# The delta rule of a two-block layer stack over chunks of 128 tokens in place of 64

## The reference

```
lower = strict_lower((beta k) k^T * decay)          # C x C
u, w  = solve(I + lower, [beta v, beta k exp(gc)])   # unit lower triangular
intra = lower_incl(q k^T * decay)
per chunk, in order:
    v_new = u - w S
    o     = (q exp(gc)) S + intra v_new
    S     = S exp(g_last) + (k exp(g_last - gc))^T v_new
```

## Time and profile before

| | |
|---|---|
| median of 3 runs | 2641.05 us |
| the profiled execution | 2638.55 us |
| its span in the profile | 2636.4 us |
| mean granted TensorE clock | 0.977 |
| TensorE matmul busy | 2543.8 us (96%) |
| VectorE busy | 1718.5 us (65%) |
| ScalarE busy | 1226.5 us (47%) |
| DMA | 428.50 MB, mean 163 GB/s |

### The profile page before, as it was taken

The page is one execution under the profiler, slowest core; times in us unless marked ns, Lnnn a source line. Parts: engine busy times, 40 slices in busy tenths (PEclk is TensorE's granted clock), DMA queues, the critical chain, the costliest instruction groups (busy, mean ns, idle before and its releaser), DMA issues.

```text
span 2636.4 us, 39407 instructions
## 1 busy us (share of the span) xinstructions
PE 2543.8 (96%) x17188; PEld 2337.9 (89%) x17188; DVE 1718.5 (65%) x1888; ACT 1226.5 (47%) x1275; POOL 0.2 (0%) x4
## 2 busy tenths in 40 slices
PE   7999999899998998999999999999899999999997
PEld 7998888789998978799999989987799999898876
DVE  5699855755888737565655657556656756577664
ACT  5544224554452225554334333337456556455573
POOL 0000000000000000000000000000000000000000
PEclk8999989999999979999999999999999999999999
DMA  5453222355442213455555555555445555545553
GB/s 209 166 178 129 96 79 89 136 192 180 175 175 95 86 61 112 165 204 179 186 183 191 178 190 188 183 201 199 159 176 176 179 189 176 185 180 179 183 193 119
DMA packets 63212, 428.50 MB, mean 163 GB/s; under 512 B 6976, under 2 KB 7104, under 8 KB 13504
## 3 DMA queue, kind: packets, MB, share of 16 engines
q1 hardware_dynamic: 60496, 414.97, 44.3%
q10 hardware_dynamic: 2544, 11.01, 1.1%
HBM read 421.76 MB, written 4.19 MB: 162 GB/s over the span
## 4 chain that ended last, share of the span: by engine, by line
PE 84%; DVE 6%; ACT 6%; issue 3%; DMA 0%; ACTq 0%; DVEq 0%; SPq 0%
PE PS L406 83%; ACT Q L878 2%; DVE Q L1456 2%; ACT WH L892 1%; DVE WL L1491 1%; PE PS L496 1%; DVE QA L1460 1%; ACT L878 1%; DVE Y L1456 1%; ACT QA L878 1%; DVE X L1460 1%; DVE Q L1460 0%; ACT HH L878 0%; PE PS L692 0%; DVE QA L1456 0%
## 5 line engine op out<-in xcount | busy, mean ns | idle before, releaser
L1491 DVE TENSOR_TENSOR WL<-W,WH 128x2048 fp32r<-128x2048 f32 (+2 forms) x388 | 861.2, 2224 | 544.1 <-ACT WH L892 544.0
L892 ACT ACTIVATE WH<-W 128x2048 fp32r<-128x2048 f32 (+2 forms) x388 | 717.5, 1858 | 779.8 <-PE PS L406 666.6
L406 PE MATMUL PS<-HH,WL 128*128 128x256 f32 x3392 | 564.2, 286 | 17.2 <-DVE WL L1491 12.1
L406 PE MATMUL PS<-HL,WH 128*128 128x256 f32 x3392 | 557.6, 284 | 0.0
L406 PE MATMUL PS<-HH,WH 128*128 128x256 f32 x3392 | 557.1, 284 | 0.0
L406 PEld LDWEIGHTS PS<-HH,WL 128*128 128x128 f32 x3392 | 474.0, 193 | 24.8 <-DVE WL L1491 12.7
L406 PEld LDWEIGHTS PS<-HL,WH 128*128 128x128 f32 x3392 | 473.3, 193 | 0.0
L406 PEld LDWEIGHTS PS<-HH,WH 128*128 128x128 f32 x3392 | 472.9, 193 | 0.0
L406 PE MATMUL PS<-WL,HH 128*128 128x512 f32 (+2 forms) x768 | 231.0, 382 | 10.0 <-DVE HL L1456 10.0
L406 PE MATMUL PS<-WH,HL 128*128 128x512 f32 (+2 forms) x768 | 223.7, 372 | 0.0
L406 PE MATMUL PS<-WH,HH 128*128 128x512 f32 (+2 forms) x768 | 222.7, 371 | 0.0
(11 more groups left out here) (135 smaller groups left out, 1990.1 us busy)
## 6 DMA issues: line engine op xcount, KB each, us to landing
W<-in_wall SPq DMA_DIRECT2D x378, 1024.0 KB, 4.8
W<-in_wall SPq DMA_DIRECT2D x16, 512.0 KB, 3.5
W<-in_wall SPq DMA_DIRECT2D x8, 536.0 KB, 3.4
X<-in_x SPq DMA_DIRECT2D x4, 512.0 KB, 7.4
X<-in_x ACTq DMA_DIRECT2D x1, 2048.0 KB, 10.2
xsave<-X ACTq DMA_DIRECT2D x1, 2048.0 KB, 10.7
X<-xsave ACTq DMA_DIRECT2D x1, 2048.0 KB, 11.0
Q<-in_g_post ACTq DMA_DIRECT2D x8, 256.0 KB, 3.3
```

The costliest lines, as they stand in the source:

```text
L406: return e.matmul(o, l, r, start=start, stop=stop, skip_group_check=True)
L892: e.activation(WH[:, s % NSPL, 0:m], W[:, c % NRAW, 0:m], ACT.Copy).then_inc(*up("hi", c))
L1491: e.tensor_tensor(WL[:, c % NRAW, 0:m], W[:, c % NRAW, 0:m], WH[:, s % NSPL, 0:m].bitcast(F32), ALU.subtract).then_inc(*up("lo", c))
```

## The change

The constants' masks lose the blocks of 64 (`cum`, `incl`, `strict`; `last` becomes `ones`), and there is a sixth level, 128. The scan has two steps: in the first S is zero, so its `v_new` is `U2` itself, its state is the product `kv` alone, copied by ScalarE, and its output is one product; the second makes `ws`, `vn` and an output of two products, and no further state. `wk`, `EG`, `CQ`, `RW` and `KD` are made only for the half that is read. TensorE's wait for `kb` ahead of `kk` stands four pumps later, the `tu` transposes two later in all, and attention's `kr` wait three pumps later on TensorE and ScalarE. VectorE's counts stay but for the sixth level and the scan.

```diff
-    same = (i[:, None] // 64) == (i[None, :] // 64)
-    c["cum"] = same & (i[:, None] <= i[None, :])
+    c["cum"] = i[:, None] <= i[None, :]
...
+        def three(ap):
+            return ap[:, 0:384].rearrange("p (h c) -> p h c", h=3)
...
-        LEVELS = (4, 8, 16, 32, 64)
+        LEVELS = (4, 8, 16, 32, 64, 128)
...
# TensorE
-                yield from rest(4)
+                yield from rest(8)
                 for k in range(3):
                     for which, rhs_ in (("kk", KB), ("kq", CQ)):
...
                     yield
-                yield from rest(4)
+                yield from rest(2)
                 for k in range(3):
                     b = side(("dn", l, "tu", k), ("dn_a", l, "tu", k))
...
-                        for which in ("u", "t") if m < 64 else ("u",):
+                        for which in ("u", "t") if m < 128 else ("u",):
...
+                for k in range(2):
+                    b = side(("dn", l, "wk", k), ("dn_a", l, "wk", k))
+                    for h in range(3 * k, 3 * k + 3):
+                        us = slice(256 * h + 128, 256 * h + 256)
+                        i = mm(b[:, 128 * (h % 3):128 * (h % 3) + 128], RW[:, us], UU[:, us], start=(h % 3 == 0))
...
                 yield from rest(2)
-                for c in range(4):
...
+                w.wait_ge(*to("dn_a", l, "uv", 2))
+                for k in range(2):
+                    b = side(("dn", l, "kv", k), ("dn_a", l, "s", k))
+                    for h in range(3 * k, 3 * k + 3):
+                        i = mm(b[:, 128 * (h % 3):128 * (h % 3) + 128], KD[:, of(0, h)], U2[:, of(0, h)],
+                               start=(h % 3 == 0))
+                    i.then_inc(*up("dn_p", l, "kv", k))
+                for k in range(2):
+                    b = side(("dn", l, "o", 0, k), ("dn_a", l, "o", 0, k))
...
+                yield from rest(3)
+                w.wait_ge(*to("dn_a", l, "s", 1))
+                for k in range(2):
+                    b = side(("dn", l, "ws", k), ("dn_v", l, "vn", k))
...
+                yield from rest(3)
+                w.wait_ge(*to("dn_v", l, "vn", 1))
+                for k in range(2):
+                    b = side(("dn", l, "o", 1, k), ("dn_a", l, "o", 1, k))
+                    for h in range(3 * k, 3 * k + 3):
+                        o = b[:, 128 * (h % 3):128 * (h % 3) + 128]
+                        hs = slice(128 * h, 128 * h + 128)
+                        mm(o, SS[:, hs], CQ[:, of(1, h)], start=(h % 3 == 0), stop=False)
+                        i = mm(o, VN[:, hs], DI[:, of(1, h)], start=False)
+                    i.then_inc(*up("dn_p", l, "o", 1, k))
+                yield from rest(4)
                 w.wait_ge(*to("dn_a", l, "oo"))
...
# attention, TensorE (ScalarE: 16 to 19)
-                yield from rest(17)
+                yield from rest(20)
                 w.wait_ge(*to("at_v", l, "kr"))
...
# ScalarE
-                yield from rest(2 * 2 + 5 * 5)
+                yield from rest(2 * 2 + 5 * 6 + 1)
...
+                for k in range(2):
+                    w.wait_ge(*to("dn_p", l, "kv", k))
+                    act(SS[:, 384 * k:384 * k + 384], sbank("dn", l, "kv", k)[:, 0:384], ACT.Copy, "dn_a", l, "s", k)
                 yield
+                out_of(0)
+                yield from rest(6)
+                out_of(1)
+                act(DI, OC, ACT.Square, "dn_a", l, "oo")
...
# VectorE
-                tt(CQ, CQ, EG, ALU.mult, "dn_v", l, "qg")
+                tt(heads(CQ)[:, :, 1, :], heads(CQ)[:, :, 1, :], heads(EG)[:, :, 1, :], ALU.mult, "dn_v", l, "qg")
...
+                    for t, dst, v, sig in ((1, RW, gs[:, 60:72], ()), (0, KD, kdw, ("dn_v", l, "tk", k))):
+                        tt(heads(dst)[:, 2 * k:2 * k + 2, t, :], quad(sbank("dn", l, "tk", k))[:, t::2, :],
...
-                for c in range(4):
...
+                for k in range(2):
+                    w.wait_ge(*to("dn_p", l, "ws", k))
+                    tt(three(VN[:, 384 * k:384 * k + 384]), heads(U2)[:, 3 * k:3 * k + 3, 1, :],
+                       three(sbank("dn", l, "ws", k)), ALU.subtract, "dn_v", l, "vn", k)
```

More of the change, by code:

```diff
@@ L110, in const_columns @@
     c["ident"] = np.eye(128)
-    same = (i[:, None] // 64) == (i[None, :] // 64)
-    c["cum"] = same & (i[:, None] <= i[None, :])
-    c["last"] = same
-    c["incl"] = same & (i[:, None] <= i[None, :])
-    c["strict"] = -1.0 * (same & (i[:, None] < i[None, :]))
+    c["cum"] = i[:, None] <= i[None, :]
+    c["incl"] = i[:, None] <= i[None, :]
+    c["strict"] = -1.0 * (i[:, None] < i[None, :])
     up = lambda m: ((i[:, None] // m) == (i[None, :] // m)) & ((i[:, None] % m) < m // 2) & ((i[None, :] % m) >= m // 2)
     c["lv2"] = up(2)
-    for m in (4, 8, 16, 32, 64):
+    for m in (4, 8, 16, 32, 64, 128):
         c[f"lv{m}"] = up(m).T
@@ L518, in decays @@
                 mm(b[:, 0:12], tbl("cum"), gs[:, 12:24])
-                mm(b[:, 16:28], tbl("last"), gs[:, 12:24], start=False).then_inc(*up("dn_p", l, "gc"))
+                mm(b[:, 16:28], ones, gs[:, 12:24], start=False).then_inc(*up("dn_p", l, "gc"))
                 for k in range(3):
@@ L593, in delta_net @@
                     yield from rest(3)
+                w.wait_ge(*to("dn_v", l, "u", 128, 2))
                 for k in range(3):
[L595 to L602, removed]
@@ L603, in delta_net @@
-                yield from rest(2)
-                for c in range(4):
[L605 to L637, removed]
@@ L638, in delta_net @@
-                yield
+                    b = side(("dn", l, "uv", k), ("dn_a", l, "uv", k))
+                    for j in range(4):
+                        us = slice(128 * (4 * k + j), 128 * (4 * k + j) + 128)
+                        i = mm(b[:, 128 * j:128 * j + 128], UU[:, us], RV[:, us], start=(j == 0))
+                    i.then_inc(*up("dn_p", l, "uv", k))
+                for k in range(2):
[3 more added lines that the diff above has]
+                        i = mm(b[:, 128 * (h % 3):128 * (h % 3) + 128], RW[:, us], UU[:, us], start=(h % 3 == 0))
+                    i.then_inc(*up("dn_p", l, "wk", k))
@@ L1089, in attention @@
                 act(sm[:, 0:32], sm[:, 0:32], ACT.Exp, "at_a", l, "rs", scale=-0.5, bias=0.0)
-                yield from rest(16)
+                yield from rest(19)
                 for k in range(5):
@@ L1731, in delta_net @@
-                yield
+                for k in range(2):
+                    w.wait_ge(*to("dn_p", l, "ws", k))
+                    tt(three(VN[:, 384 * k:384 * k + 384]), heads(U2)[:, 3 * k:3 * k + 3, 1, :],
+                       three(sbank("dn", l, "ws", k)), ALU.subtract, "dn_v", l, "vn", k)
+                yield from rest(9)
                 w.wait_ge(*to("dn_a", l, "onr"))
```

67 lines of the change are left out of this document (28 added, 39 removed).

## The result

The kernel after takes 2565.28 us in the median of 4 runs (2563.20 to 2567.36), beside 2639.47 (2635.18 to 2643.32) for the kernel before: a ratio of 0.9719, 95% interval 0.9701 to 0.9737. Its profiled execution took 2567.36 us with a span of 2565.4, which is 71.0 less than before. The forecast was 2571, with a range of 2555 to 2596.

The account below looks back on a forecast made before the run. TensorE, busy 96% of the span, was taken as the bound, in the scan with a swinging clock. 48.9 + 6.6 + 8.3 + 6.5 = 70.3 us off 2638.55 gave 2568.3, or 2571 against the median 2641.05; range 2555 to 2596.

Parts of the forecast that it names:

- The `kb` wait: Ahead of kk: TensorE's wait, moved four units later, mostly goes with its slow clock; 6.6 us layer 0, 8.3 layer 1.
- Level and scan: From uv/wk to the norm: fewer, full matmuls, sixth level included, 47.4 us a layer against 71.20 and 72.48; 48.9 won.
- The 2.8 us for a fall of the clock behind it: At the norm behind the 2.10 us wait: allowance a layer for a clock fall, added to 44.6, giving 47.4.
- Rival A: Scan and early waits: the clock stays low as before, so the kernel takes 2583 to 2591 us; chance 0.20.
- The step's reason: Old scan: small matmuls cost more than full ones, 0.185 to 0.19 us a record against 0.110, through array-mode changes.
- Attention: Attention's start, kr wait three units later: 3 + 3.5 = 6.5 us won over both layers, bounded by -2 and 10.
- the end of the stage: Attention's last transposes, layer 0: they come when they came, but with two units more done, 2.8 us.
- B: At tk, level 4, norm and attention: more waits and clock falls go, 17 us more won, 2554; chance 0.14.
- C: VectorE's queue, standing ahead of TensorE, delays taps and WL splits; 87 us paid against 70 won, 2658; chance 0.03.
- D: Scan: small products are covered beside the units, so only waits go and levels cost 15.8 us, 2635; chance 0.03.

Follow-up runs that it names:

- grouped: Kernel before, 64 tokens a step, with each step's twelve output products ordered as six of 128 rows, then six of 64: 2617.28 us, ratio 0.9921.
- mixed: Kernel after with only the last output product in the old form, 64 columns wide, 128-row and 64-row products in turn: 2587.64 us, ratio 0.9805.
- sorted: Kernel mixed with its 48 records of output 1 reordered, in each bank 128-row products first, then 64-row ones: 2578.08 us, ratio 0.9772.
- cols64: Kernel after with each of the 30 scan matmuls a layer made as two of 64 columns, all with 128 rows: 2581.42 us, ratio 0.9781.
- rows64: Kernel after with each of the 30 scan matmuls a layer summed over rows 0 to 63 only, 128 columns wide: 2570.93 us, ratio 0.974.
- soon: Kernel after with ScalarE's first attention exponentials one pump later, so that it splits Y ahead of them: 2563.68 us, ratio 0.972.
- best: Kernel soon with ws and the output of step 1 one and two units earlier on TensorE, against the kernel after: 2563.38 us, ratio 0.972.

## Why the prediction was right, and where it was not

**The `kb` wait (6.6 + 8.3).** Right in size and in place. In layer 0, `kk` came at 246.44 without a wait (246.7 forecast) and `tu` at 258.98 (259.0); the new waits were 2.66 and 1.35 (2.8 and 1.2 forecast). VectorE's `tv` products started 2.3 us sooner (2.2 forecast) and its `tk` products took 1.6 less (1.9 forecast). In layer 1 of the profiled execution the wait at `tk` was 2.27 and the clock behind it did fall, to 0.50 from 797.06 to 800.00; the first `u`/`t` then had nothing to wait for, and the part came out at 8.1. Put back the wait costs 10.0 us, less than the 14.9 forecast for the part; the rest, 2.5 us of layer 0's 6.7, most likely comes from VectorE's shorter products, which no run took alone. That the move is no step of its own was not seen: in the kernel before it wins hardly anything that can be told.

**Level and scan (48.9).** Right, 2 to 3 us a layer too careful. All 128x128 records took 0.11, the level 7.3 us a layer (7.9 forecast), the wait ahead of the norm stayed at 2.10. The 2.8 us for a fall of the clock behind it came in the profiled layer 0 in part (4.25 against 2.85 us for the norm's records) and not at all in layer 1: that is most of the careful part. Whether they come differs between executions, so this much of the hit is luck. Rival A, the clock staying low, fell with the 0.94 and 1.00.

**The step's reason.** The size of the price was read rightly from the earlier trace rows, its owner half rightly. It isn't that the products are small: 64 columns alone cost 0.11 and 64 rows alone 0.12. The alternation makes 0.184 of 0.126; the clock's falls came where 64-row products of 64 columns stood beside 128-row ones, in whatever order. Size and sign of the forecast didn't depend on this, since the change removes both.

**Attention (6.5).** The one term that was mis-sized: 3.3 by the ledger, 2.9 by putting it back. The wait for HL came out at 4.97 (5.5 forecast), as argued. The step that was too large is the end of the stage: two units more done behind the last transposes, 2.8 us. The two units did stand ahead of them, but TensorE waited 2.43 us there in both layers (0.82 and 1.54 before), and the clock fell behind that wait; first before, with three units there, then after, with one.
```profile
514.41:518.69 4.28, 4.28 (x21) 1.00 0.39 105
```
```profile
482.88:485.62 2.74, 2.74 (x10) 0.52 0.44 72
```
So from the last transposes to the next wait for HL only 1.35 us were won in each layer (11.83 to 10.48). The transposes themselves, which should have come when they came, came 0.9 us later in layer 0 and 1.6 sooner in layer 1, counted from the end of the norm. Together that is the 0.4 and 2.9 of the ledger. All of layer 0's waits in attention sum to 9.76 us before (with 0.27, 2.03 and 1.85 beside those of the earlier trace rows) and to 9.45 after. In layer 1 they fell from 13.05 to 9.44, and with attention's start put back they are 12.31 and 13.26. So the move takes waits away, and layer 0 of the kernel before had few to lose; why, stays open.

**The rivals.** Of B's extra winnings, in layer 1 the wait at the first level and the fall of the clock behind the norm went; the rest did not come. C, VectorE's queue, did not come: TensorE's idle for WL is 12.1 us after and before. D fell with the scan.

**What stays open.** Why the clock falls. With TensorE busy it fell only in or behind the scans and outputs of before, grouped, mixed and sorted, where products of 64 rows and 64 columns stand beside products of 128 rows. It did not fall over the records of 64 columns with 128 rows (cols64), nor over those of 64 rows with 128 columns (rows64, 1.00 in both layers); in the traces of these two, and of every other kernel here without such products, each fall from 1.00 stands behind a wait. So neither the columns nor the rows alone do it, and the number of 64-row records doesn't either: rows64 has 24 of them in a row, and in sorted only 12 had gone by when the clock fell, for 35 records were made by 385.53 and they come as 12 of 128 rows, 12 of 64, 12 of 128. Whether it takes both at once, or 64 and 128 rows within one bank, no run here tells. Behind an idle of 2.1 us the clock fell in some executions and not in others of one and the same kernel.

## What to carry to other kernels

- Look at the price of one record at the full clock, shape by shape. Where operands of 64 and of 128 rows take turns, group them first: here an edit of the order alone won 22 us of 2639, without any new algorithm. An fp32 matmul of half the rows or half the columns saved nothing here (0.12 and 0.11 us a record against 0.11), so fill the array.
- Before taking away a wait, ask which engine's chain sets the next place at which they meet. A wait removed ahead of a stage that VectorE paces came back within it (soon, best, and the `kb` move alone), while work removed from TensorE where TensorE is the bound came out nearly in full (7.3 of 7.9 us for the level).
- Price a wait with the clock behind it: TensorE ran at 0.50 behind the wait of 4.97 us and at 1.00 behind the one of 1.67, and that is where soon's 1.5 us show.
- Price steps in the kernel in which they will stand: the same moved wait was worth 10 us after the change and 2 before it.

## What the hardware showed unexpectedly

- An fp32 record of 64 columns takes what one of 128 takes, 0.11 us (48 in 5.46 us); one with 64 rows 0.12 (24 in 2.94 us).
- Operands of 128 and 64 rows in turn: 0.184 us a record, the same records grouped: 0.126, both at 2.4 GHz (0.16 against 0.11 in mixed and sorted).
- The granted clock fell from 1.00 to 0.50 within the 48 records of sorted while TensorE was never idle; over the 24 records of 64 rows and 128 columns of rows64 it was 1.00.
- An idle of 2.10 us was followed by a lower clock in layer 0 of one execution of the kernel after and by 1.00 over the next records in both layers of another.
